# Multiplying constants into a free PSUM bank in the pauses of six layer norms

## The reference

```
kv = mem @ mem_w_kv
for i in range(2):
    y = mlstm_mixer(x, ...) if i == 0 else pool_mixer(x, ...)
    x = layer_norm(ALPHA * x + y, ln_g[i, 0], ln_b[i, 0])
    x = layer_norm(ALPHA * x + memory_cross_attn(x, ...), ln_g[i, 1], ln_b[i, 1])
    x = layer_norm(ALPHA * x + sq_relu_mlp(x, ...), ln_g[i, 2], ln_b[i, 2])

layer_norm(x) = (x - mean(x)) * rsqrt(mean((x - mean(x))**2) + 1e-5) * g + b
```

## Time and profile before

| what | value |
|---|---|
| median of 3 runs | 3493.74 us |
| profiled execution | 3496.58 us, its span 3494.8 us |
| mean granted TensorE clock | 0.928 of full speed |
| TensorE matmuls busy | 2945.1 us (84%) |
| VectorE busy | 2257.4 us (65%) |
| GpSimd busy | 1856.1 us (53%) |
| ScalarE busy | 926.1 us (26%) |

### The profile page before, as it was taken

The page is one execution under the profiler, slowest core; times in us unless marked ns, Lnnn a source line. Parts: engine busy times, 40 slices in busy tenths (PEclk is TensorE's granted clock), DMA queues, the critical chain, the costliest instruction groups (busy, mean ns, idle before and its releaser), DMA issues. The chain is left out here.

```text
span 3494.8 us, 33128 instructions
## 1 busy us (share of the span) xinstructions
PE 2945.1 (84%) x10628; PEld 1938.5 (55%) x10628; DVE 2257.4 (65%) x3761; ACT 926.1 (26%) x2350; POOL 1856.1 (53%) x1099
## 2 busy tenths in 40 slices
PE   6889898877778877888877779979899975889998
PEld 5667676632333323444433267657678864667886
DVE  7793464376666667776766583675855577586556
ACT  2115402233433333333333322221200012220001
POOL 2544375464444444666554264254577763557874
PEclk9899899999999999999999989989999987999998
DMA  5531122699999999999999811011122220112221
GB/s 216 185 113 55 43 79 73 241 421 419 413 418 412 412 422 409 391 389 399 390 422 418 341 66 55 31 60 61 60 90 96 91 72 12 61 60 93 94 96 55
DMA packets 126107, 719.21 MB, mean 206 GB/s; under 512 B 13200, under 2 KB 16400, under 8 KB 60176
## 3 DMA queue, kind: packets, MB, share of 16 engines
q0 software_dynamic: 73728, 536.90, 37.4%
q1 hardware_dynamic: 46560, 161.18, 13.4%
q10 hardware_dynamic: 5680, 19.40, 1.5%
HBM read 715.33 MB, written 2.10 MB: 205 GB/s over the span
## 5 line engine op out<-in xcount | busy, mean ns | idle before, releaser
L712 PE MATMUL psum<-slots,acc 128*128 128x512 f32 x2048 | 1016.2, 643 | 267.9 <-ACT acc L1167 267.4
L398 POOL TENSOR_TENSOR whi<-w,zeros 128x1024 fp32r<-128x1024 f32 x277 | 548.1, 1979 | 883.1 <-PE psum L469 566.4
L428 POOL DMA_INDIRECT slots<-in_experts,consts x512 | 564.1, 1102 | 675.0 <-PE psum L712 603.5
L1719 DVE SCALAR_TENSOR_TENSOR arena<-slots,work 128x1024 f32<-128x1024 f32 x512 | 663.2, 1295 | 400.1 <-DMA slots<-in_experts,consts 383.1
L712 PEld LDWEIGHTS psum<-slots,acc 128*128 128x128 f32 x2048 | 393.7, 202 | 868.5 <-ACT acc L1167 462.3
L401 POOL TENSOR_TENSOR wlo<-w,whi 128x1024 fp32r<-128x1024 f32 x277 | 718.2, 2593 | 21.7
L467 PE MATMUL psum<-xhi,whi 128*128 128x512 f32 x1104 | 451.5, 409 | 8.7 <-POOL wlo L401 5.6
L468 PE MATMUL psum<-xlo,whi 128*128 128x512 f32 x1104 | 441.8, 400 | 0.0
L469 PE MATMUL psum<-xhi,wlo 128*128 128x512 f32 x1104 | 440.5, 399 | 0.0
L467 PE MATMUL psum<-yhi,whi 128*128 128x512 f32 (+1 forms) x736 | 300.1, 408 | 49.9 <-POOL ylo L453 20.7
L468 PE MATMUL psum<-ylo,whi 128*128 128x512 f32 (+1 forms) x736 | 296.2, 402 | 0.0
(11 more groups left out here) (266 smaller groups left out, 3671.3 us busy)
## 6 DMA issues: line engine op xcount, KB each, us to landing
w<-in_stream SPq DMA_DIRECT2D x277, 512.0 KB
arena<-in_wmod SPq DMA_DIRECT2D x4, 2048.0 KB, 17.8
arena<-in_wmod ACTq DMA_DIRECT2D x8, 1024.0 KB, 6.1
acc<-in_wmod ACTq DMA_DIRECT2D x8, 1024.0 KB, 8.3
slots<-in_experts,consts POOLq DMA_INDIRECT x512
xres<-in_xT SPq DMA_DIRECT2D x1, 2048.0 KB, 15.3
outT<-xres SPq DMA_DIRECT2D x8, 256.0 KB, 2.0
consts<-in_consts SPq DMA_DIRECT2D x1, 1056.0 KB, 5.2
```

The source lines that it names most:

```text
L398: pool.tensor_tensor(hi, w32[:, s, :], zeros[:, :].broadcast_to((P, 1024)), ALU.add)\
L428: pool.indirect_dma_start(out=slots[p % SLOTS], out_offset=None, in_=a["experts"], in_offset=bass.IndirectOffsetOnAxis(ap=indices[:, p:p + ...
L712: mm = pe.matmul(bank(4 + half), diag[:, p % 2, :], v[:, half * T:(half + 1) * T], start=(c == 0), stop=(c == PICKS - 1))
L1719: dve.scalar_tensor_tensor(dot_out, slots[p % SLOTS][:, 0:D], 1.0, tokens[:, p // PICKS, :], ALU.mult, ALU.mult, accum_out=inner[:, c:c + ...
```

## The change

TensorE gets a helper, `keep_busy`, that multiplies the identity matrix with the first 256 columns of the constants (the identity and the ones) a number of times, in fp32, into the first 256 columns of bank 7. Nobody reads the result. It waits for nothing. It is called at two places: ahead of the wait for `summed` in the norms with a mean, 4 to 9, 12 times in norms 5 and 8 and 20 times in the others; and, in the same norms, 4 times between the spread of the means and the wait for `root_ready`.

```diff
+            def keep_busy(count):
+
+                for _ in range(count):
+                    pe.matmul(bank(7)[:, 0:2 * P], ident, consts[:, 0:2 * P], start=True, stop=True)
+
             def norm_sums(ni, cols=T, mean=False):
 
+                if mean:
+                    keep_busy(12 if ni == 5 or ni == 8 else 20)
                 pe.wait_ge(sem("summed"), 8 * (ni + 1))
...
             def norm_spread(ni, cols=T, to=5):
+                if ni > 3:
+                    keep_busy(4)
                 pe.wait_ge(sem("root_ready"), ni + 1)
                 spread(bank(to), stats[ni % 2][:, 0:4], cols).then_inc(sem("inverse_spread"), 1)
```

## The result

The changed kernel took 3503.92 us (median of 6 runs, 3501.52 to 3507.2), the kernel before 3492.47 beside it: ratio 1.0032, 95% interval 1.0019 to 1.0045, so 11 us slower. Measured once more beside another set of runs of before (the last experiment), the ratio was 1.0018, 1.0009 to 1.0028, 6 us. The profiled execution took 3501.52 (span 3499.7), 4.9 more than that of before.

A forecast was written before the change was run, and what follows sets the result against it. VectorE's running sums end TensorE's pauses; only the clock behind them can change. Norms 4 to 9 at +1.45, -1.3, +0.95, +1.05, -1.3, +5.5 give +6.4 us, from 3493.74 to 3500.1; range 3489 to 3508.

The forecast's parts named there:

- main term: Norm 9, ahead of the sums: 20 calls, 8.83 us, meet a pause of 2.90 us and delay the path by 5.9 us.
- Norm 9 as a whole: Norm 9: +5.9 us for the block, -0.4 for the sums, 0 for the calls between the spreads; +5.5 together.
- The pauses of norms 4 to 8: Ahead of the sums: constants fit into VectorE's pauses and cost nothing, leaving 0.8 to 4.4 us empty.
- The four calls between the spreads: Between the spreads: -0.35 us at full clock, +3.1 at low, +1.45 in norms 4, 6, 7, +0.2 in 5, 8, 0 in 9.
- The sums and spreads of norms 5 and 8: Norms 5 and 8: sums at full clock -1.5 us each, spreads +0.2 each; -1.3 each.
- The product groups: Products behind the norms: the 3.35 us wait for the first tile stays empty, so the clock drops; costed at 0.
- a sign of being wrong: Product groups: the prediction is wrong if the clock is at full speed under them.
- A: Rival, all norms: the high clock holds through every norm; -10.1 us, 3483.6 us; chance 0.09.
- B: Rival: sums count as work, so norms 5 and 8 are held from end to end; +2.3 us, 3496.0 us; chance 0.14.
- C: Rival, between the spreads: the four calls meet a low clock in every norm; +18 us, 3511.7 us; chance 0.10.
- 3.5 us of scatter: Whole kernel: the forecast's spread, about 3.5 us either way, as the clock's falls and rises differ between executions.

The follow-up runs named there:

- the last experiment: The unaltered change measured again beside another set of runs of the kernel before: ratio 1.0018, +6.3 us.
- ahead only: The change without the four calls between the spreads, keeping the constants ahead of the sums: ratio 1.0005, +1.7 us against the kernel before.
- the block in norm 9 alone: The kernel before with 20 constants ahead of the sums of norm 9 and no other calls: ratio 1.0015, +5.2 us against the kernel before.
- without block 9: The change without the 20 constants ahead of the sums of norm 9, all others kept: ratio 1.0005, +1.7 us against the kernel before.
- with five calls: The change with 5 constants instead of 20 ahead of the sums of norm 9: ratio 1.0007, +2.4 us against the kernel before.

## Why the prediction was right, and where it was off

**Direction and main term: right.** It forecast 3500.1, slower by 6.4, and gave "within 0.2%" the larger chance (0.50, against 0.40 for slower); 3503.9 is in the range of 3489 to 3508. The first measurement lies beyond 0.2%, the second just inside it. The largest term, 20 calls of 0.44 us in a pause of 2.9 us, is the largest in the runs too: +5.2 by itself, and gone when the calls are cut to five. A call took 0.44 us (40 records in 8.79).

**Norm 9 as a whole: near by luck.** It was forecast at +5.5 and is +6.48 in the trace, but it is made up otherwise. The block by itself is smaller, 4.2 us in "ahead only" and 4.55 alone: the sums came 5.6 us late, and then not only the sums (0.5) but also both spreads and the centring (0.9 in "ahead only") went faster at the full clock. The four calls between the spreads, which the forecast put at 0 here, cost the other 2.3 (28.26 against 25.97 us in "ahead only"). The forecast took norm 9's clock to be full at the spreads; it fell 0.3 us into the first.

**The pauses of norms 4 to 8: right.** None of the sums is late; 0.95 us is left in norms 5 and 8 (0.8 forecast).

**The four calls between the spreads: right in mechanism, too small in size.** With a full clock scaling starts 3.82 us after the first spread (3.75 forecast, 4.10 before); low, 5.5 to 6.7. I had taken 3.8 us from the spreads' start to the rise for all norms. It was 3.6 in norm 4, but 4.9 in norm 7 and 5.5 in norm 6 (2859.06 to 2864.6), so norm 6 paid 2.42 in place of 0.95. In norm 8 it was 5.2. The rows of before that I averaged over, spreads without anything between them, do not say how long the clock stays low when a pause ends at another moment.

**The sums and spreads of norms 5 and 8: half right.** I gave both the same -1.3. Norm 5 was held and gained 1.90; in norm 8, with the same pause and the same 0.95 us behind the constants, the clock fell at 3086.6, 1.3 us into the sums, and it lost 1.19. The mean of an even chance was near neither.

**The product groups: right on average only.** I costed them at 0 since the hole of 3.35 us in front of them stays. It did not stay: with the second spread later it is 2.9 us. In norms 4 and 5 the groups ran at full clock (-1.33 and -1.46 behind the first scaled tile), which the prediction had named as a sign of being wrong; in norm 7 they were low for 6.0 us (+2.36), in norm 8 as before (-0.13): -0.6 together. That this came out near 0 is luck. The +2.36 cannot be put down to the change, since the kernel with the block in norm 9 alone has +2.45 at the same place without a call. That the hole is what matters is shown by the calls put into it.

**The rivals.** A (the clock holds through everything) is refuted by five norms of six. Its terms add up to -10.2, not -10.1; without norm 9's block they are -16, and with the pauses filled and the hole too -12.2 came by the runs. B (norms 5 and 8 held from end to end) came in norm 5 and failed in norm 8. C (low under all spreads, +18) did not come. Its sign, a rise later than 5.1 us after the spreads' start, did come, in norms 6 (5.5) and 8 (5.2), but not its price: from the start of the spreads on these two lost 2.4 and 2.2 us, where C had 3.1. One reading of the earlier trace rows was too wide: a wait followed by a cold start is there in five norms of before, not in six; in norm 9 the sums began at the full clock after an idle 2.90 us.

**Chance.** I took 3.5 us of scatter between executions from the clock in these norms. Four traces (the change, the change again, without block 9, with five calls) agree in all five stretches from norm 4 to norm 8 within 0.1 us, and what differs between them lies before norm 4. But the traces of before and of the block alone, which also do the same work up to norm 8, differ there by 3.3 us, all of it in norms 7 and 8. So part of the scatter does come from the clock in these norms, as the forecast had it; how much, two and four traces do not say.

## What to carry to other kernels

A filler on a waiting engine is worth what stands behind it: size each block to its own pause in the trace (here 12, 20 and 20 met pauses of 6, 12 and 2.9 us), put it in front of the wait that it fills and never between two steps of a chain that others wait for. Fill the last hole before the dense work first; 24 calls there gained 5.9 us, the same number one step earlier cost 4.9, and filling only the earlier pauses moves the low clock into the dense work. Compare two traces from the last point that the change cannot reach, and look at a second trace of unchanged work before you read a difference of 2 us in one stretch.

## What the runs showed of the hardware

- A pause of 2.9 us in front of the same work could leave TensorE's clock full or not: in the change it was full after an idle 2.91 and 2.90 us in norms 4 and 5, low in norms 7 and 8 after 2.91.
- The clock fell while matmuls of one column ran and stayed full in another norm with the same work: in norm 8 of the change it fell 1.3 us into the sums, with 5.34 us of constants ending 0.95 us ahead of them; in norm 5, with the same 12 calls and the same 0.95 us, it stayed.
- The pattern of falls and rises can repeat from execution to execution and need not. Four kernels with the same work from norm 4 to norm 8, starting at 2293.0, 2294.5, 2294.6 and 2300.1 us, have stretch lengths equal within 0.1 us. Two others with the same work there (before and the block in norm 9 alone, starting at 2299.7 and 2294.8) differ by 2.5 us in the stretch of norm 7, by a low clock of 2.8 and of 6.1 us behind the same hole. And five calls ahead of norm 9's sums left the clock full through the first spread in one kernel (last stretch 21.13 us) and not in another with the same work (24.21).
